# Router products with the router's matrix stationary, and another order for attention's first head

## The reference, cut to what matters

```python
u2 = modulate(rmsnorm(h, norm_ffn_g), sh2, sc2)
scores = sigmoid(u2 @ w_router)            # 512 x 1024 by 1024 x 64
choice = scores + router_bias              # then the top 4 of 8 groups, the top 8 experts
```

```python
proj = xn @ w_in                           # q and gate, from rms_norm(h, norm_pre)
q = partial_rope(proj[..., :D]) * Dh ** -0.5 ; gate = proj[..., D:]
kv = rms_norm(h, kv_norm) @ kv_w           # k and v, from another norm of the same h
k = partial_rope(kv[..., :D]) ; v = kv[..., D:]
```

## Time and profile before

| | before |
|---|---|
| median of 3 runs | 2959.12 us (2957.44 to 2965.87) |
| the profiled execution | 2953.93 us, its span 2952.6 us |
| PE busy | 2699.3 us, 91% of the span |
| DVE, ACT, POOL busy | 35%, 24%, 6% |
| PE's share of the chain that ended last | 75%, DMA 10%, DVE 6%, ACT 5% |
| mean granted clock of PE | 0.958 of full speed |

### The profile page before, as it was taken

How to read it: one execution, slowest core, us unless ns; L and a number is a source line. 1 busy time by engine, 2 the same in 40 slices (tenths; PEclk the granted TensorE clock), 3 DMA queues, 4 the chain that set the end, 5 groups by cost and what they waited for, 6 DMA issues and landing times.

```text
span 2952.6 us, 41816 instructions
## 1 busy us (share of the span) xinstructions
PE 2699.3 (91%) x17136; PEld 1588.6 (54%) x17136; DVE 1038.8 (35%) x2273; ACT 701.6 (24%) x1144; POOL 166.5 (6%) x128
## 2 busy tenths in 40 slices
PE   8999999999998899998998899969996969999797
PEld 3666665444447576666655344357773425545443
DVE  4565664322212322222211501056771132433312
ACT  2333332100012111111111201145552122333311
POOL 0000000000000122222222000000000000000000
PEclk9999999999998899999999899979998989999799
DMA  6322211433322999998998332120112121111110
GB/s 249 114 86 76 81 65 32 160 128 128 130 74 111 382 323 385 344 393 324 392 339 302 133 139 89 68 108 25 46 32 109 42 80 57 43 43 57 37 42 29
DMA packets 81997, 428.12 MB, mean 145 GB/s; under 512 B 16240, under 2 KB 16752, under 8 KB 39184
## 3 DMA queue, kind: packets, MB, share of 16 engines
q1 hardware_dynamic: 53872, 368.47, 31.9%
q0 software_dynamic: 18096, 37.80, 5.0%
q10 hardware_dynamic: 9840, 19.17, 1.8%
HBM read 394.88 MB, written 58.79 MB: 154 GB/s over the span
## 4 chain that ended last, share of the span: by engine, by line
PE 75%; DMA 10%; DVE 6%; ACT 5%; issue 2%; SPq 0%; POOL 0%; ACTq 0%; DVEq 0%; POOLq 0%
PE psum_all L281 35%; PE psum_all L1989 7%; PE psum_all L1482 7%; PE psum_all L3424 4%; PE psum_all L2177 4%; DMA big<-t_experts 4%; PE psum_all L1529 4%; PE psum_all L3297 3%; PE psum_all L291 3%; DMA total_rows<-big,rows 2%; DMA weights<-t_experts 2%; DMA weights<-t_ada 1%; PE psum_all L306 1%; PE psum_all L677 1%; DVE big L3558 1%
## 5 line engine op out<-in xcount | busy, mean ns | idle before, releaser
L281 PE MATMUL psum_all<-u,weights 128*128 128x512 f32 x1024 | 448.6, 595 | 12.3 <-issue 12.3
L281 PE MATMUL psum_all<-big,weights 128*128 128x512 f32 (+1 forms) x768 | 340.3, 599 | 11.3 <-DVE big L953 6.4
L281 PEld LDWEIGHTS psum_all<-u,weights 128*128 128x128 f32 x1024 | 193.2, 191 | 244.4 <-issue 243.9
L281 PEld LDWEIGHTS psum_all<-big,weights 128*128 128x128 f32 (+1 forms) x768 | 145.4, 190 | 200.8 <-issue 194.2
L1989 PE MATMUL psum_all<-big,weights 128*128 128x512 f32 x512 | 223.0, 598 | 6.1 <-DVE big L2082 4.9
L1482 PE MATMUL psum_all<-big 128*32 128x256 f32 (+2 forms) x1648 | 196.5, 387 | 9.4 <-DMA big<-t_experts 8.0
L1482 PE MATMUL psum_all<-weights,big 128*64 128x256 f32 (+2 forms) x1296 | 192.6, 406 | 11.1 <-DMA weights<-t_experts 10.7
L1989 PEld LDWEIGHTS psum_all<-big,weights 128*128 128x128 f32 x512 | 98.2, 192 | 130.8 <-issue 128.0
L1482 PEld LDWEIGHTS psum_all<-weights,big 128*64 128x64 f32 (+2 forms) x1296 | 133.8, 150 | 54.3 <-issue 21.5
L281 PE MATMUL psum_all<-weights,u 128*128 128x256 f32 (+1 forms) x704 | 153.5, 383 | 9.6 <-ACT u L457 9.6
L1482 PEld LDWEIGHTS psum_all<-big 128*32 128x32 f32 (+2 forms) x1648 | 137.9, 134 | 43.5 <-issue 12.7
(11 more groups left out here) (370 smaller groups left out, 3360.2 us busy)
## 6 DMA issues: line engine op xcount, KB each, us to landing
big<-t_experts SPq DMA_DIRECT2D x96, 1024.0 KB
weights<-t_experts SPq DMA_DIRECT2D x96, 1024.0 KB
weights<-t_ada SPq DMA_DIRECT2D x24, 1024.0 KB, 6.9
weights<-t_rkvg SPq DMA_DIRECT2D x16, 1024.0 KB, 6.8
rwkv_inputs<-big ACTq DMA_DIRECT2D x48, 256.0 KB, 2.0
big<-rwkv_inputs SPq DMA_DIRECT2D x8, 1280.0 KB, 7.1
weights<-t_x SPq DMA_DIRECT2D x8, 1024.0 KB, 5.0
weights<-t_BC SPq DMA_DIRECT2D x8, 1024.0 KB, 5.1
```

Source lines behind the costliest of these rows:

```text
L281: last = pe.matmul(out, lhsT, rhs, start=n == 0, stop=n == len(terms) - 1)
```

## The change

The router's 8 matrix tiles (128 channels by 64 experts) go into the array and u moves through it, 512 columns at a time, as soon as each tile of u is there. Even tiles k use the array's columns 0 to 63 and accumulate on PSUM partitions 0 to 63 of bank 5, odd ones columns 64 to 127 and partitions 64 to 127. ACT copies bank 5 to `K.sq[0]`; 4 products with a token tile of that copy in the array and the 64-column constant `eye64` (two identities, one above the other) turned through it add the two halves and put tokens on the partitions, in bank 4 as before. The sigmoid waits for these. In the attention, head 0's projections are taken out of the loop into `first_head_pe` and `first_head_act`: q follows the tiles of u one by one, then gate, the rotation of q, k (bank 5) following the tiles of hk, half of v, the rotation of k, the rest of v. DVE marks each tile of u for this.

```diff
 def router_pe(K, X, q, qu, w):
     pe, wt = K.nc.tensor, K.W.tile(w, KD, E_ALL)
-    pe.wait_ge(*qu.act.at("u", KD - 1))
     pe.wait_ge(*K.W.here(w))
+    K.bank(5, q.act, "score halves")
+    for k in range(KD):
+        pe.wait_ge(*qu.act.at("u", k))
+        ins = pe.matmul(K.psum[half(k % 2), 5, :], wt[:, k, :], K.u[:, k, :], start=k < 2, stop=k >= KD - 2)
+    ins.then_inc(*K.W.left(w, q.pe))
+    pe.wait_ge(*q.act.at("score halves"))
     K.bank(4, q.act, "score")
     for t in range(NT):
-        ins = products(pe, K.psum[:, 4, t * E_ALL:(t + 1) * E_ALL], [(tile(K.u[:, k, :], t), wt[:, k, :]) for k in range(KD)])
-    ins.then_inc(*K.W.left(w, q.pe))
+        ins = pe.matmul(K.psum[:, 4, t * E_ALL:(t + 1) * E_ALL], tile(K.sq[0], t), K.c("eye64"), start=True, stop=True)
+    ins.then_inc(*q.pe.tick("score"))
...
 def router_act(K, A, X, q, before, w):
...
     act.wait_ge(*q.pe.at("w", w))
+    act.activation(K.sq[0], K.psum[:, 5, :], ACT.Copy).then_inc(*q.act.tick("score halves"))
+    act.wait_ge(*q.pe.at("score"))
     act.activation(X.score.rearrange("p a b -> p (a b)"), K.psum[:, 4, 0:NT * E_ALL], ACT.Sigmoid) \
...
+def first_head_pe(K, X, q, w0):
+    pe, wq, wk = K.nc.tensor, two_tiles(K, w0, KD, P), two_tiles(K, w0 + 1, KD, P)
+    pe.wait_ge(*K.W.here(w0))
+    K.bank(6, q.act, "q", 0)
+    for k in range(KD):
+        pe.wait_ge(*q.dve.at("u", k))
+        ins = pe.matmul(K.psum[:, 6, :], wq[:, 0, k, :], K.u[:, k, :], start=k == 0, stop=k == KD - 1)
+    ins.then_inc(*q.pe.tick("q", 0))
+    K.bank(7, q.act, "gate", 0)
+    products(pe, K.psum[:, 7, :], column_terms(wq[:, 1], 0, K.u)).then_inc(*K.W.left(w0, q.pe))
+    rope_pe(K, X, q, 0, "q", X.q[0])
+    pe.wait_ge(*K.W.here(w0 + 1))
+    K.bank(5, q.act, "k", 0)
+    for k in range(KD):
+        pe.wait_ge(*q.dve.at("hk", k))
+        ins = pe.matmul(K.psum[:, 5, :], wk[:, 0, k, :], X.hk[:, k, :], start=k == 0, stop=k == KD - 1)
+    ins.then_inc(*q.pe.tick("k", 0))
+    K.bank(7, q.act, "v", 0)
+    values_pe(K, X, q, 0, wk[:, 1], (0, 1))
+    rope_pe(K, X, q, 0, "k", X.k[0])
+    values_pe(K, X, q, 0, wk[:, 1], (2, 3)).then_inc(*K.W.left(w0 + 1, q.pe))
+
+def first_head_act(K, X, q, w0):
+    act = K.nc.scalar
+    act.wait_ge(*q.pe.at("q", 0))
+    act.activation(X.q[0], K.psum[:, 6, :], ACT.Copy, scale=HEAD ** -0.5).then_inc(*q.act.tick("q", 0))
+    act.wait_ge(*q.pe.at("w", w0))
+    act.activation(X.gate[0], K.psum[:, 7, :], ACT.Silu).then_inc(*q.act.tick("gate", 0))
+    act.wait_ge(*q.pe.at("k", 0))
+    act.activation(X.k[0], K.psum[:, 5, :], ACT.Copy).then_inc(*q.act.tick("k", 0))
+    act.wait_ge(*q.pe.at("w", w0 + 1))
+    act.activation(X.v[0], K.psum[:, 7, :], ACT.Copy).then_inc(*q.act.tick("v", 0))
...
@@ attention_pe
-        if f == 0:
-            pe.wait_ge(*q.dve.at("hk", KD - 1))
@@ attention_start_dve
-                .then_inc(*(q.dve.tick("hk", k) if dst is X.hk else q.dve.tick()))
+                .then_inc(*q.dve.tick("hk" if dst is X.hk else "u", k))
@@ attend
-    for s in range(-1, KD + 1):
+    first_head_pe(K, X, q, w)
+    first_head_act(K, X, q, w)
+    for name, dst in (("q", X.q[0]), ("k", X.k[0])):
+        rope_dve(K, X, q, 0, name, dst)
+    for s in range(KD + 1):
```

## The result

| | median | runs | profiled execution's span |
|---|---|---|---|
| before | 2959.87 us | 2957.44 to 2965.87, 4 runs | 2952.6 us |
| after | 2929.95 us | 2924.22 to 2930.64, 4 runs | 2929.0 us |

The ratio is 0.9892 (95% interval 0.9872 to 0.9911): 29.9 us faster. The forecast was 2937.7, 21.4 us faster, with a range from 2931 to 2948.

The account below looks back on a forecast made before the run. PE, busy 91% of the span with 75% of the chain, was taken to bound the kernel, including its waits for norms. Router 11.5 plus attention 9.9 made 21.4 us, 2959.12 to 2937.7; range 2931 to 2948.

Parts of the forecast that it names:

- Router, 11.5 us: Router: 16 half-array passes following u replace 64 small passes, so PE reaches the shared products earlier by 11.5 us.
- the case that the prediction worked out first: Router: clock rises at 890.3, PE reaches the shared products at 897.8 where it was at 909.77, 12.0 us.
- the table load: Router: ACT's sigmoid table load, 1.28 us, now behind the copy, costs 0.2 us of ACT.
- Attention, 9.9 us: Attention's first head: PE starts at DVE's first tile of u instead of after all 16, gaining 9.9 us.
- The cover: Behind the router: DVE's choice of experts ended at 916.69, `count_pe` comes at 937.5, 21 us of cover; both move together.
- the shift passes through whole: Experts' stage: weight stream and its use both start earlier, so the router's gain reaches the end undiminished.
- the 5.2 us between the profiled execution and the median: Whole kernel: the runs' median, 2959.12 us, lies 5.2 us above the profiled execution, 2953.93; forecast given in the runs' terms.
- (a): Router: clock does not rise in the halves; router gain 6.6 to 8.8 us, total about 17.5, 2941.6; chance 0.17.
- (b): Router: the two array halves do not run side by side; total gain 11.8 to 18.8 us, about 2943; chance 0.10.
- (c): Experts' stage: weight stream swallows the router's gain, only attention's 9.9 us stays, 2949.2; chance 0.06.
- (d): Shared expert: clock stays at 1.2 GHz from the halves through its 128 passes; 11.3 us slower, 2970.4; chance 0.03.
- (e): Both parts: something else holds PE at the first tile, so both give little, 2957; chance 0.02.

Follow-up runs that it names:

- set 1: Router's part alone, attention's part alone, and the changed and unchanged kernels again, beside the kernel before: 2939.05, 2948.25, 2928.58 and 2958.19 us against 2958.39.
- third look at after: The changed kernel, unchanged, run once more beside its padded version with 79 more PE instructions: 2928.28 us.
- after + 79: Changed kernel with 79 more PE instructions (158 satisfied waits) at the head of the joining step, run twice: 2933.84 and 2935.24 us.
- before + 177 in two lots: Kernel before with 177 more PE instructions (satisfied waits), 100 at the joining step and 77 ahead of the loop over pairs: 2950.13 us, ratio 0.9974.
- set 3: Runs beside the kernel before (2958.83 us): changed kernel 2928.28, the same with 79 more PE instructions 2935.24, kernel before with 177 more in two lots 2950.13.
- set 2: Runs beside the kernel before (2960.06 us), among them the changed kernel with 79 more PE instructions: 2933.84 us, ratio 0.9921.
- one half: Changed kernel with all 8 router tiles in array columns 0 to 63, one after the other: 2932.99 us, ratio 0.9909.
- second of before: Second profile of the kernel before, unchanged, run as a control: 2958.19 us, ratio 1.0001.
- head alone: Kernel before with only attention's part of the diff, router as before: 2948.25 us, ratio 0.9956.
- warmed head: Changed kernel with 4 products without use ahead of attention's q, in PE's idle time: 2926.59 us, ratio 0.9892.

## Why the prediction was right, and where it was wrong

**Router, 11.5 us (6.6 to 12.0).** Measured 12.0, the case that the prediction worked out first and then took 0.5 off for a later rise of the clock. The rise was put at 890.3 and came at 891.2, with everything in after 0.67 us later than in before, so 0.2 us off. The passes ended 0.8 us later than put (893.3, of which 0.67 is the shift), the table load cost what it was given, and the transposes took 3.66 for 3.7.

**Attention, 9.9 us (8.3 to 10.4).** Measured 9.8 between the first two profiles and 10.2 in set 1; in the third look at after the stretch was 33.6 us long instead of 32.2, so 8.5. The first pass comes 0.90 us after DVE starts, not 0.75, and q has the two low-clock tiles that were foreseen.

**What lies between and behind.** The cover held: the shared products take 27.79 us as before, 67.1 us pass from their start to the first expert (67.4 before), and the attention behind the first scores takes 488.0 against 487.7.

**The step that failed** is the sentence on which the sum rests, that DVE, POOL and SP work through what PE releases and that "the shift passes through whole". It looked at engines, queues and the weight stream, and counted the 40 products saved, but it took the rest of PE's program as unmoved and so put the RWKV stage at nothing in the sum. The program is itself something that streams in. With the borders moved the stage takes 475.0 us instead of 480.6 in the profiles' means, a term of 5.6 to 6.2 us, and by the medians of the padded kernels moving the borders is worth 7.0 us (after beside after + 79) and 8.7 (before beside before + 177 in two lots).

With the profiles' term the sum is 12.0 + 9.8 + 5.6 to 6.2 = 27.4 to 28.0 us, against 29.9, 29.8 and 30.6 where after ran beside before. The last 1.8 to 3.2 us I can't place; with the router's edit the experts' stage differs by 6 us from profile to profile, and medians of 4 to 6 runs move by 1 to 2. The other way to part the terms is to compare kernels whose borders lie alike. In the new position after is 21.9 us faster than before + 177 in two lots (2928.28 and 2950.13, both in set 3); in the old one after + 79 is 23.6 us faster than before in set 3 and 26.2 in set 2. So the 21.4 us were near the worth of the two edits by themselves, and the missing step is the moving of the borders.

The row that shows it could have been read beforehand: the gaps at 1960.49 and 1994.95 stand in the trace of before, called issue. But that they would go and not move to a place as bad could only be guessed, so the honest use would have been a wider range, by some 6 us on either side, and a forecast near the same.

**The range** also carried the 5.2 us between the profiled execution and the median. The two profiled spans differ by 23.6 us: 12.0 + 9.8 + 2.4 in the RWKV stage (478.0 and 475.6, a long one of the new and the shortest of the old) and small terms of both signs. On the profiled executions the forecast's 21.4 looks good; on medians the whole 6 us show. One profile of each kernel would have hidden the missing term.

**The rivals.** (a) fell: the clock rose within the halves, before the first transpose, so its case of 6.6 us was not put to the test. (b) fell, by the 3.0 us that one half costs. The rule of the Trainium skill named beside it ("TensorE: Matmul & The Clock Gate", Part 3), that weight loads overlap running matmuls only where the row group differs, does not hold for these passes: in after a load runs from 889.55 to 889.73 beside a pass on the same rows from 889.39 to 890.45. (c) fell: the experts' stage passed the shift through, within its scatter. (d) fell: no us at half clock between the rise at 891.2 and the end of the shared products. (e) fell: PE's first pass comes 0.86 us after ACT's start.

## What to carry to other kernels

An edit that changes the number of instructions on an engine moves the borders of its program's pieces in all that follows; where that engine runs short instructions without slack, a border cost 0.3 to 2.7 us here, and the six longest gaps came with a fall of the clock, so price each such stage at some microseconds in both directions. To know what an edit itself is worth, put the missing instructions back as waits in an idle stretch, and compare that kernel. Look for idle time called issue in the middle of a row of like instructions, with an instruction packet that starts 2 to 3 us before its end, and count whether such gaps lie a multiple of 256 instructions apart.

## What the runs showed of the hardware that I had not expected

A gap of 2.44 to 2.45 us at the same pass in five profiles, 2.71 in a sixth, of four programs whose borders lie alike. In the eight profiles of those where they lie otherwise no gap at a border is over 0.99 us. (All fourteen have one more of 12.2 to 12.4 us called issue near the stage's end, which lies at no border.) All 45 gaps at borders end 2.2 to 2.9 us after the start of a packet of PE's program, so what a border costs is how long before that moment PE has run out of instructions. Why some of these packets start so late that PE is already idle is open.

The gap is not all of the cost. In all six profiles with the long gap the clock fell to 1.2 GHz near its end, from 0.5 us before PE resumed to 2.0 us after, for 3.4 us or more. In three profiles the clock also fell for 3.4 us with no border's gap near, 2.0 to 2.7 us after a wait of 1.15 us for ACT (at 1976.40 in the second of before, 1980.71 in the head alone, 1968.12 in the warmed head), so not every low stretch of the table comes from a border.

Both are seen in a stage in which PE gets through some 20 to 40 passes of 64x64 in a microsecond; in the other stages no gap of 0.3 us or more called issue stands at a border in any of the fourteen profiles.

A satisfied wait is cheap but not free: with 100 instructions of two waits at the head of the joining step PE's idle time there was 16.39 us, with 177 it was 24.93, which is 0.11 us for each of the 77 more. And after the router's 64 passes of 64 columns the clock was still at 0.50 after 13.9 us, while it rose 3.5 us into the passes that use only half of the array.
